# Expert rows are scaled by their share as they leave PSUM, and ten accumulating gathers add them to the residual

## What the reference computes

```python
w_top = softmax(top_v) * p_grp                    # two experts a token, inside its best group
combine = sum(one_hot(expert_id, 16) * w_top)     # 544 x 16, two numbers a row are not zero
for e in range(16):
    h = silu(xn @ w_gate[e]) * (xn @ w_up[e])     # 1024 -> 256
    out = out + combine[:, e] * (h @ w_down[e])   # 256 -> 1024
x = x + out
```

## Time and profile before

| | |
|---|---|
| median of 3 runs (lowest, highest) | 1452.21 us (1451.4, 1453.23) |
| the profiled execution: its time, its span | 1452.92 us, 1450.8 us |
| PE busy | 1375.2 us (95%) |
| DVE busy | 787.6 us (54%) |
| ACT busy | 637.0 us (44%) |
| POOL busy | 89.1 us (6%) |
| mean granted TensorE clock | 0.983 of full speed |
| bytes over DMA | 228.27 MB, 160 GB/s of HBM over the span |

### The profile page before, as it was taken

The page is one execution under the profiler, slowest core; times in us unless marked ns, Lnnn a source line. Parts: engine busy times, 40 slices in busy tenths (PEclk is TensorE's granted clock), DMA queues, the critical chain, the costliest instruction groups (busy, mean ns, idle before and its releaser), DMA issues.

```text
span 1450.8 us, 20873 instructions
## 1 busy us (share of the span) xinstructions
PE 1375.2 (95%) x8370; PEld 1119.2 (77%) x8370; DVE 787.6 (54%) x1155; ACT 637.0 (44%) x932; POOL 89.1 (6%) x88
## 2 busy tenths in 40 slices
PE   7998999999999999999789999999999999999995
PEld 6994666899999766767579846668999997666763
DVE  4427545443435357887553285465343443678876
ACT  5327645522224245565333375454222242456551
POOL 0310000000000011010203000000000000101002
PEclk9999999999999999999879999999999999999998
DMA  8233300023215349998812203001233163699955
GB/s 247 88 106 107 117 1 0 30 88 116 82 63 218 148 186 387 410 413 296 259 59 73 67 3 117 0 1 30 87 116 108 37 247 129 231 397 409 409 212 199
DMA packets 97384, 228.27 MB, mean 157 GB/s; under 512 B 16459, under 2 KB 66661, under 8 KB 84326
## 3 DMA queue, kind: packets, MB, share of 16 engines
q1 hardware_dynamic: 85222, 179.42, 34.3%
q0 software_dynamic: 7904, 32.64, 6.2%
q10 hardware_dynamic: 4176, 15.08, 2.6%
HBM read 198.56 MB, written 33.79 MB: 160 GB/s over the span
## 4 chain that ended last, share of the span: by engine, by line
PE 83%; DVE 6%; ACT 5%; DMA 3%; issue 2%; SPq 1%; ACTq 0%; DVEq 0%; PEldq 0%; POOLq 0%
PE ps L864 10%; PE ps L866 10%; PE ps L865 10%; PE ps L1353 7%; PE ps L1329 4%; PE ps L1331 4%; PE ps L1330 4%; PE ps L890 3%; PE ps L893 3%; PE ps L896 3%; PE ps L1158 2%; PE ps L1214 2%; PE ps L1216 2%; PE ps L1215 2%; PE ps L1314 2%
## 5 line engine op out<-in xcount | busy, mean ns | idle before, releaser
L1896 DVE TENSOR_TENSOR work<-work,ps 128x544 f32<-128x544 f32 x48 | 34.6, 721 | 208.8 <-ACT work L1709 208.8
L1709 ACT ACTIVATE work<-ps 128x544 f32<-128x544 f32 x48 | 30.0, 625 | 244.8 <-PE ps L866 244.8
L865 PE MATMUL ps<-xn_r,ksv_r 128*128 128x272 f32 x384 | 110.8, 289 | 0.0
L865 PE MATMUL ps<-xn_r,work_r 128*128 128x272 f32 x384 | 110.8, 288 | 0.0
L777 POOL DMA_INDIRECT rows_back<-xrow_d,row_of x32 | 34.4, 1075 | 1093.3 <-DVE row_of L2272 867.8
L1331 PE MATMUL ps<-ew_r,rows_tok_r 128*128 128x512 f32 x256 | 99.9, 390 | 0.0
L1896 DVE TENSOR_TENSOR ew_r<-ew,gu_hi_a_r 128x2048 fp32r<-128x2048 f32 x32 | 73.3, 2290 | 17.3 <-ACT gu_hi_a_r L1732 17.1
L865 PEld LDWEIGHTS ps<-xn_r,ksv_r 128*128 128x128 f32 x384 | 72.2, 188 | 0.0
L865 PEld LDWEIGHTS ps<-xn_r,work_r 128*128 128x128 f32 x384 | 72.2, 188 | 0.0
L1732 ACT ACTIVATE gu_hi_a_r<-ew 128x2048 fp32r<-128x2048 f32 x32 | 60.6, 1908 | 5.6 <-ACT yo_b L1779 5.6
L1353 PE MATMUL ps<-ew,acts 128*128 128x512 f32 x128 | 57.9, 595 | 3.6 <-DVE acts L2403 3.6
(11 more groups left out here) (405 smaller groups left out, 3881.9 us busy)
## 6 DMA issues: line engine op xcount, KB each, us to landing
wr<-in_w_in SPq DMA_DIRECT2D x68, 512.0 KB, 4.8
ew<-in_w_exp_gate SPq DMA_DIRECT2D x32, 1024.0 KB, 6.6
ew<-in_w_exp_up SPq DMA_DIRECT2D x32, 1024.0 KB, 10.2
ew<-in_w_exp_down SPq DMA_DIRECT2D x32, 1024.0 KB, 9.6
wr<-in_w_out SPq DMA_DIRECT2D x16, 512.0 KB, 4.4
rows_d<-yo_a ACTq DMA_DIRECT2D x14, 512.0 KB, 8.2
rows_d<-yo_b ACTq DMA_DIRECT2D x14, 512.0 KB, 8.4
rows_d<-in_zeros POOLq DMA_DIRECT2D x10, 512.0 KB, 9.4
```

Source lines behind the costliest of these rows:

```text
L865: mm(out_[h], w_hi, x_lo[:, c], start=False, stop=False, skip_group_check=True)
L1896: return v_.tensor_tensor(o_, a, b, op)
```

## The change

ACT multiplies each expert row by its share as the row leaves PSUM, so the rows in DRAM are final. For that, DVE makes a table of 16 shares a token (`shares`) at expert 0, SP writes it to DRAM (`shares_d`), and POOL gathers from it, for each expert, 128 rows of 64 bytes into one of four slots of `w_rows`; column e of it is the share. The ten gathers at the end of a layer no longer go to buffers: they add straight into `xres[t]` (`compute_op=ALU.add`), first one slot for all five tiles, then the other, each tile's second after its first has landed. `gathered` is gone. Slots of the last two experts now point to a row of zeros. The fp16 parts of the last experts' weights are gone too.

```diff
 def gathered(l, t):                                   # the whole function is removed
-    dve.wait_ge(gath[t][0], at(gath[t], l, 32))
-    v_.scalar_tensor_tensor(out=xres[t][0:m, :], in0=g1[t][0:m, :], scalar=r_w1[0:m, t:t + 1], in1=xres[t][0:m, :], ...)
-    v_.scalar_tensor_tensor(out=xres[t][0:m, :], in0=g2[t][0:m, :], scalar=r_w2[0:m, t:t + 1], in1=xres[t][0:m, :], ...)
 def placed(l, t, banks_):
-    dve.wait_ge(cb_1[0], at(cb_1, l, 2 * t + 2))
+    dve.wait_ge(gath[t][0], at(gath[t], l, 32))
...
 # POOL, end of a layer
-pool.wait_ge(gu_mm[0], at(gu_mm, l, NE - 1))
-for t in range(NTILE):
-    for w, g in enumerate((g1, g2)):
-        pool.indirect_dma_start(g[t][0:TM[t], :], None, rows_d, ...slots[0:TM[t], w * NTILE + t]...).then_inc(gath[t][0], 16)
+pool.wait_ge(fn_x[0], at(fn_x, l, NTILE))
+for w in range(2):
+    for t in range(NTILE):
+        if w:
+            pool.wait_ge(gath[t][0], at(gath[t], l, 16))
+        pool.indirect_dma_start(xres[t][0:TM[t], :], None, rows_d, ...slots[0:TM[t], w * NTILE + t]...,
+                                compute_op=ALU.add).then_inc(gath[t][0], 16)
...
 # POOL, loop over experts: after gather(e) comes the gather of the shares of e - 2
+def gather_shares(e):
+    pool.wait_ge(spill[0], at(spill, l, spill[1]))        # the table is in DRAM
+    pool.wait_ge(w_in[0], at(w_in, l, 16 * e))
+    if e >= WS:
+        pool.wait_ge(yo_ev[0], at(yo_ev, l, e - WS + 1))
+    pool.indirect_dma_start(w_rows[:, e % WS, :], None, shares_d, ...row_of[:, e:e + 1]...).then_inc(w_in[0], 16)
...
 # SP, ahead of the loop that loads the weights of experts 4 to 15
+sp.wait_ge(shares_rdy[0], at(shares_rdy, l, 1))
+sp.dma_start(shares_d..., shares...).then_inc(spill[0], 16)
...
 # ACT
 def rows_done(n, s):
+    if isinstance(n, int):
+        act.wait_ge(w_in[0], at(w_in, l, 16 * n + 16))
-    f(yo[s]..., ps[:, 4 + 2 * s:6 + 2 * s, :], ACT.Copy).then_inc(yo_ev[0], 1)
+    f(yo[s]..., ps[:, 4 + 2 * s:6 + 2 * s, :], ACT.Copy,
+      scale=w_own[n] if isinstance(n, int) else w_spare[:, s:s + 1]).then_inc(yo_ev[0], 1)
...
 # DVE, loop over experts
-if e == 5: expert_shares()
-if e == 6: weights_of_last(); weight_part(0)
-if e == 8: weight_part(1); weight_part(2)
-if e == 10: shares_kept()
-if e == NE - 2: slot_weights()
 if e == 0:
+    expert_shares()
     one_hot(4)
 # expert_shares gets three instructions more, of 128x80: the table of shares
+    ins = tt(by_te[w], oh12[:, w]..., r_w.unsqueeze(2).to_broadcast([P, NTILE, NE]), ALU.mult)    # w = 0, 1
+    tt(shares, shares, r_dif, ALU.add).then_inc(shares_rdy[0], 1)
 # slots_kept gets one small instruction more, spare_tables (e == 13) two:
+    link(v_.tensor_scalar(r_ei, r_ei, float(P), None, ALU.mult))
+    link(tt(r_own, e128..., r_ei..., ALU.is_equal))
```

More of the change, by code:

```diff
@@ L281, in hybrid_streaming_encoder @@
         fss, frs = small[:, 58:63], small[:, 63:68]
-        w_slot, w_parts, keep = small[:, 88:90], small[:, 128:134], small[:, 140:150]
+        w_spare, keep = small[:, 88:90], small[:, 140:150]
+        w_own = [w_rows[:, e % WS, e:e + 1] for e in range(NE)]
         ps = ctx.enter_context(nc.psum_tensor("ps", [P, 8, 512], F32))
@@ L455, in hybrid_streaming_encoder @@
         gath = [sem(f"gath{t}", 32) for t in range(NTILE)]
-        cb_1 = sem("cb_1", 2 * NTILE)
+        w_in = sem("w_in", 16 * NE)
         cmb_mm = sem("cmb_mm", 1 + NTILE)
@@ L697, in _ @@
                 load_down(l, 3, 3)
+                sp.wait_ge(shares_rdy[0], at(shares_rdy, l, 1))
+                stand(sp)
+                sp.dma_start(shares_d.rearrange("(t p) e -> p t e", p=P), shares.rearrange("p (t e) -> p t e", t=NTILE)).then_inc(spill[0], 16)
                 for e in range(NE):
@@ L778, in gather @@
                                             bass.IndirectOffsetOnAxis(ap=row_of[:, e:e + 1], axis=0)).then_inc(xg_in[e % 2][0], 16)
+                def gather_shares(e):
[3 more added lines that the diff above has]
+                        pool.wait_ge(yo_ev[0], at(yo_ev, l, e - WS + 1))
+                    stand(pool)
+                    pool.indirect_dma_start(w_rows[:, e % WS, :], None, shares_d,
+                                            bass.IndirectOffsetOnAxis(ap=row_of[:, e:e + 1], axis=0)).then_inc(w_in[0], 16)
                 pool.wait_ge(spill[0], at(spill, l, 16 + 16 * NTILE))
@@ L782, in _ @@
                     gather(e)
+                    if e >= 2:
+                        gather_shares(e - 2)
+                for e in range(NE - 2, NE):
+                    gather_shares(e)
                 pairs = pairs_in_use(pool, l)
@@ L1789, in rows_up @@
                 def rows_up(i, halves_):
+                    act.wait_ge(w_in[0], at(w_in, l, w_in[1]))
                     act.wait_ge(dn_mm[0], at(dn_mm, l, TAIL + i + 1))
@@ L1929, in _ @@
                     rows_landed(range(1, NTILE))
-                if l:
-                    gathered(l - 1, 1)
                 for t in range(NTILE):
@@ L1940, in _ @@
                     if l and t + 2 < NTILE:
-                        gathered(l - 1, t + 2)
                         placed(l - 1, t + 2, JOINT_BANKS)
@@ L1957, in _ @@
                     v_.tensor_copy(ident_h[:, :], ident).then_inc(dve_fills[0], 1)
-                    for i in range(2):
-                        v_.tensor_copy(tok_w[:, i, :, 0], con[:, K_TOK:K_TOK + 5]).then_inc(dve_fills[0], 1)
                 dve.wait_ge(smalls[0], at(smalls, l, 304))
@@ L2317, in slots_kept @@
                     link(v_.scalar_tensor_tensor(out=keep, in0=r_slot, scalar=float(P * NE) - 0.5, in1=keep, op0=ALU.is_gt, op1=ALU.add))
-                    link(tt(r_pos[:, 0:10], r_slot, keep, ALU.mult))
+                    link(v_.scalar_tensor_tensor(out=r_pos[:, 0:10], in0=r_slot, scalar=-float(P * TAIL), in1=keep, op0=ALU.add, op1=ALU.mult))
+                    link(v_.tensor_scalar(r_pos[:, 0:10], r_pos[:, 0:10], float(P * TAIL), None, ALU.add))
                     v_.tensor_copy(slots[:, :], r_pos[:, 0:10]).then_inc(slots_rdy[0], 1)
@@ L2459, in _ @@
                             v_.tensor_copy(row_of[:, NE + s:NE + s + 1], ps[:, 2 + s, 508:509]).then_inc(idx_ev[0], 1)
+                        dve.wait_ge(xsp_in[l][0], it * 64 + 64)
+                        dve.wait_ge(yo_ev[0], at(yo_ev, l, n - 2))
+                        for s in range(2):
+                            own = r_own[:, bass.ds(it * 2 + s, 1), :].rearrange("p o e -> p (o e)")
+                            tt(r_far[:, NE * s:NE * s + NE], w_rows[:, s, :], own, ALU.mult).then_inc(eh_g[0], 1)
+                        dve.wait_ge(eh_g[0], at(eh_g, l, it * 4 + (NE + 2)))
+                        for s in range(2):
+                            v_.tensor_reduce(w_spare[:, s:s + 1], r_far[:, NE * s:NE * s + NE], AX, ALU.add)
                         for s, i in enumerate(SPARE_SLOTS):
```

101 lines of the change are left out of this document (29 added, 72 removed).

## The result

The changed kernel takes 1456.42 us in the median of 8 runs (1452.9 to 1459.15), the kernel before 1451.95 us in the runs beside it (1449.37 to 1453.58). The ratio is 1.0031, its 95% interval 1.0021 to 1.0041: 4.5 us slower, where 4 us faster was forecast. The profiled execution took 1459.15 us, its span is 1457.1. In the third group of experiments one execution of `g9_tiles_first` (2278.71 us) and one of the kernel before (1969.72 us) were slow, at a granted clock of 0.56 and 0.65 instead of 0.98, and stay out of the ratios.

The account below looks back on a forecast made before the run. PE was taken to bound the loop, DVE the end, and slice 1 of `w_in`, held up by gathers, plus DVE the passage. Terms: +6.8 - 2.6 - 2.3 - 5.9 = -4.0 us, giving 1448.2 us; 8-in-10 range 1441 to 1461.

Parts of the forecast that it names:

- The price of a row: Accumulating gathers, DMA engines: a 4 KB row takes 0.265 us of an engine, against 0.152 for a plain one.
- the accumulating gather is dear: Rival, both places: above 0.297 us a row the change loses; at 0.35, +6.7 us, 1458.9; chance 0.26.
- my formula: With p the row price: 60 (p - 0.152) and -4.9 between the layers, 66 p - 23.4 at the end.
- the rival in which the slice isn't held back: Between the layers: slice 1 gets two turns a row and lands as before, 1441.4 us; chance 0.20 with low-price case.
- the split of slice 1: Between the layers: slice 1 of `w_in` finishes only when the gathers do, 6.8 us later; ACT's split at 726.5.
- the products ahead of `placed` of tile 2: Between the layers, DVE: both products of `gathered(2)` leave the path, 2.6 us saved.
- PE's gap: Between the layers: gap shrinks from 3.63 to 1.0 us, so tile 1's product runs at 2.4 GHz, 2.3 us saved.
- the slice's wait to cover that of `placed` of tile 0: Between the layers: gathers of tiles 0 to 2 land before slice 1, so its wait covers the wait for their `placed`.
- At the end: After the last expert: DVE's products leave the chain, last `placed` ends at 1442.6 instead of 1448.46, 5.9 us saved.
- expert 3's rows: Experts' loop: gather issued behind the first shares, landing in up to 10.4 us, at 564, before PE's 565.52; cover 1.5 us.
- loads land 10 us before they are needed: Experts' loop: weight loads have this slack, so 128 packets of 64 bytes more an expert count as nothing.
- ACT waiting for shares: Sign against the forecast: it is wrong if ACT ever waits for shares.

Follow-up runs that it names:

- third group of experiments: Four kernels with the gathers between the layers in another order, beside the kernel before (1453.33 us): medians 1447.34 to 1453.19 us.
- g9_tiles_first: Changed kernel, between the layers both gathers of tiles 0 to 2 first, tiles 3 and 4 after slice 1 of `w_in` lands: 1453.19 us, 1.0001 of before.
- e2_acc_const: Changed kernel without shares table write or gathers of shares, each row scaled by constant 0.3, accumulating gathers kept: 1457.07 us, 1.0034 of before.
- f6_acc_pass: `e1_plain` with accumulating gathers between the layers alone, plain ones at the end: 1458.0 us, 1.004 of before.
- e3_order: Changed kernel with expert 3's rows gathered ahead of the first shares, all gathers of shares one expert later: 1464.38 us, 1.0079 of before.
- f7_slice_first: Changed kernel with the second five gathers between the layers held until slice 1 of `w_in` has landed: 1462.1 us, 1.007 of before.
- f5_acc_end: `e1_plain` with accumulating gathers straight into x at the end of layer 1 alone: 1453.52 us, 1.0006 of before.
- e1_plain: Changed kernel with scaled rows, but plain gathers into buffers and two DVE additions a tile: 1453.3 us, 1.0003 of before.
- h1_shares_twice: `e1_plain` with each gather of shares issued twice, the second into a buffer nobody reads: 1465.3 us, 1.0089 of before.
- h4_plain_again: `e1_plain` unaltered, run once more: 1453.31 us, 1.0011 of before.

## Why the prediction was wrong, point by point

**The price of a row was the step that failed.** I took 0.265 us and got 0.326. The plain base was too low: 0.152 came from dividing the queue's time by its 184 packets, but the 0.64 MB of the earlier trace rows are only 156 rows of 4 KB, which makes 0.875 x 2 x 16 / 156 = 0.179; alone on the engines a plain row takes 0.170 to 0.189. And I took nine tenths of the serial sum for overlap that wasn't there: 0.179 + 0.125 = 0.304 with the store's rate of the earlier trace rows, and 0.326 is above even that. This fits reads that go one after the other, but no run separates them. My own break-even was 0.297, and the case "the accumulating gather is dear" (0.26) is what happened; with it at 0.35 I had written 1458.9. With 0.326 my formula gives +3.7 us, with 0.179 as its base +2.0, and 4.5 and 2.8 were measured. That this is so near is in part luck: the loops' loss isn't in the formula, and by stages its terms at 0.326 are +5.5 and -1.9 where about +4.1 and -0.5 came.

By the ratio 1.93 that the Trainium skill gives for collectives (Collectives: The Full Stack, section "The bandwidth ceiling: the fold count and why AG ≠ RS ≠ AR"), the plain row of 0.170 us would take 0.328, an estimate. The trace agrees: it shows 0.326, a factor of 1.92, where both gathers fill the engines; against 0.189, in the stretch where the plain ones don't, it is 1.72. That the sum by that ratio in the prediction stayed on the side of a gain (-0.8 us) was the too low base again.

**Between the layers.** The mechanism held: the queues take turns by packets, a row that is added is one packet, and the rival in which the slice isn't held back is out. +6.8 us was forecast for the split of slice 1; the two pairs of profiles give 34.8 - 27.2 = 7.6 and 36.6 - 27.3 = 9.3, and 60 rows x (0.326 - 0.179) would be 8.8. Over the other profiles with adding gathers in this order it varies: 36.6 us from the copy to the split in `e2_acc_const`, 32.5 in `f6_acc_pass`, 30.9 in `e3_order`. Of the gains, -2.6 for the products ahead of `placed` of tile 2 came (7.55 instead of 10.24 us), and PE's gap was 0.55 us with the next block 2.89 us long instead of 5.26, -2.4. But whether the next tile's products run at 1.2 or 2.4 GHz is not the change's doing, as the last section shows; nearly by that alone the passage of before is 71.2 us in one profile and 68.3 in the other. Over two profiles each it became 4.1 us longer; the sum of my terms was +1.9.

I had counted on the slice's wait to cover that of `placed` of tile 0. It does, but barely. Where the slice is no hindrance (`f7_slice_first`, `g9_tiles_first`) ACT's copy of the turned tile starts 6.68 us after that `placed` (735.72 - 729.04, 724.28 - 717.60). In the changed kernel that would be 721.31 + 6.68 = 727.99, and the copy starts at 730.20: had the slice been on time, the copy would have come 2.2 us earlier and no more (4.1 us by the same sum in the second profile). So the dear rows hold back both, and the slice alone is not the cause of the loss.

**At the end.** -5.9 us was forecast and -0.5 came in the span. Tile 3's second gather was to land 22.8 us after the first one's start and took 1451.78 - 1424.39 = 27.4: 66 x 0.061 = 4.0 us of price, and 0.5 us because the fixed part of a landing is longer. The first landing took 6.4 us; less 8 x 0.326 that is 3.8 instead of 3.3. The rest is small: the first gather starts 4.8 us after ACT's last copy instead of 4.6, and the span ends 2.9 us after the last addition instead of 2.4. `f5_acc_end`, 0.2 us above `e1_plain`, confirms that the end gives nothing.

**What I costed at nothing.** The `expert_shares` step at expert 0 stayed under its cover: DVE's gap there is 0.34 us instead of 1.96, and expert 2 is turned on time. Two covers failed. That of expert 3's rows was to be 1.5 us; in layer 0 the rows landed 12.1 us after their issue instead of within 10.4, and PE turned them 0.5 and 1.1 us late in the first profile, on time in the second. And I had written that loads land 10 us before they are needed. That was wrong from the rows of before already: ACT splits an up load 12.1 us after its issue, and in that stretch of layer 1 loads landed after up to 10.4 us, so the cover was 1.7 us; with the shares they land after up to 14.5 us. Together the loops lost 3.6 us in the first profile and 3.1 in the second, of which 1.7 were lost ahead of the shares, so 1.4 are left. What lengthens the landings, the 128 packets of 64 bytes an expert or the row gathers that are issued at other moments, no run separates.

**ACT waiting for shares** was named as what would prove me wrong. In the changed kernel the wait is there (1.96 us at expert 0 of layer 0), but before ACT waited 1.91 us for PE in the same place; it costs up to 0.2 us. It has no slack, though, as `e3_order` and `h1_shares_twice` show.

**The sum with the measured terms**, from the stages of two profiles each: loops +3.4 (2.5 without what was lost ahead of the shares), passage +4.1, end -0.5, 7.0 us (6.1); the medians say 4.5 and 2.8 us. Both profiled executions of after are the slowest of their series (1459.15 of 1452.9 to 1459.15, and 1465.24 of 1451.05 to 1465.24), so the stages overstate; which of them is shorter in the others isn't known.

## What to carry to other kernels

An accumulating gather moves work from an engine to the DMA engines, here at 1.7 to 1.9 times the time of a plain row: count it where those engines are what ends last, and see what else is in their queues. Give it only where the DMA engines would stand idle. In this kernel half of the rows was the better choice at the end: one plain gather, one that adds into its buffer, and one addition took 4.3 us off the end where two adding gathers took 0.5. A transfer that takes turns with a burst is as late as the burst is long, so issue what is needed last after it; and a price per row is got from bytes, not from packets.

## What the runs showed of the hardware that was not expected

An accumulating indirect gather of 128 rows holds GpSimd for 1.54 us where a plain one takes 0.94, and the next one starts 1.86 us later instead of 1.24. A gather of 128 rows of 64 bytes costs GpSimd as much as one of 4 KB rows (0.95 us), and in the loop, from 600 to 700 us, it lands after 8.8 us in the median, the rows of 4 KB after 9.3. So its bytes don't set that; that it is what stands before it in the queue fits, but no run separates it.

The same kernel can be 3 us apart in one passage, nearly all of it by TensorE's clock. PE in the first profile of the kernel before and in the second, tile 2's product after the same gap of 2.20 us:

```profile
747.86 2.05 PE L890 MATMUL ps<-work_r,qt_ht_r 128*128 128x256 f32 x8 [2.20 <-ACT qt_ht_r L1464]
```

```profile
746.62 1.18 PE L890 MATMUL ps<-work_r,qt_ht_r 128*128 128x256 f32 x8 [2.20 <-ACT qt_ht_r L1464]
```

The granted clock was 0.50 in the one stretch and 1.00 in the other (1.2 and 2.4 GHz). In the product before it, after a gap of 3.63 us in both, it had come back later in the first: from 738 to 740 us it was 0.50 there and 0.83 in the second, whose product had begun 1.0 us earlier. The turn of the next tile's rows that follows begins 62.8 us after ACT's last copy in the first profile and 59.9 in the second, which is the whole difference of the passage. And ahead of the experts' loop, where `e1_plain` and `h4_plain_again` are the same kernel, PE turns expert 0 at 534.9 us in the one and at 541.6 in the other. A single profile doesn't give the price of such a passage to better than that.
